# Sample rows of retention and state space laid out by head and token, and their state updates in sets of four

## What is computed

```python
def retention_chunk(S, q, k, v, log_gamma):            # 4 heads, dk = dv = 128, a state S for each sequence
    ...
    scores = jnp.einsum('bnhd,bmhd->bhnm', q, k) * decay[None]
    intra = jnp.einsum('bhnm,bmhe->bnhe', scores, v)
    cross = jnp.einsum('bnhd,bhde->bnhe', q * q_decay[None, :, :, None], S)
    S_new = jnp.exp(log_gamma * C)[None, :, None, None] * S + \
        jnp.einsum('bmhd,bmhe->bhde', k * k_decay[None, :, :, None], v)
    return S_new, intra + cross                         # then normalised per head, times silu(gate)

def ssd_chunk(h, x, dt, a, Bm, Cm):                     # 8 heads x 64, state 128
    ...
    cross = jnp.einsum('bnhs,bhps->bnhp', Cm, h) * jnp.exp(cum)[..., None]
    w = jnp.exp(cum[:, -1:] - cum) * dt
    h_new = jnp.exp(cum[:, -1])[:, :, None, None] * h + jnp.einsum('bmhp,bmhs->bhps', x * w[..., None], Bm)
    return h_new, intra + cross                         # then + D x, times silu(z), grouped RMSNorm
```

## Time and profile before

| what | value |
|---|---|
| time, median of 3 runs | 3921.76 us (3918.91 to 3924.99) |
| the profiled execution | 3920.59 us |
| its span, first to last instruction | 3918.7 us |
| TensorE busy, mean granted clock | 3511.9 us (90%), 0.931 |
| VectorE busy | 1735.5 us (44%) |
| ScalarE, GpSimd busy | 727.9 us (19%), 244.7 us (6%) |
| DMA | 365.8 MB, 93 GB/s over the span |

### The profile page before, as it was taken

The page is one execution under the profiler, slowest core; times in us unless marked ns, Lnnn a source line. Parts: engine busy times, 40 slices in busy tenths (PEclk is TensorE's granted clock), DMA queues, the critical chain, the costliest instruction groups (busy, mean ns, idle before and its releaser), DMA issues. The chain is left out here.

```text
span 3918.7 us, 45141 instructions
## 1 busy us (share of the span) xinstructions
PE 3511.9 (90%) x18090; PEld 2454.4 (63%) x18090; DVE 1735.5 (44%) x3249; ACT 727.9 (19%) x1550; POOL 244.7 (6%) x250
## 2 busy tenths in 40 slices
PE   5988899998988788999989889998988886989998
PEld 2643455576666566888846345555766674868887
DVE  2146295134545523454512653940445364144543
ACT  1222222111322200000012222221213221010000
POOL 0000321200100000000000004112000000000000
PEclk9989899888998889999999899997989997999999
DMA  3211355522314031222222114436231321212221
GB/s 118 86 60 39 109 180 169 179 88 91 108 39 131 25 100 44 86 86 70 70 93 92 39 49 153 159 134 223 83 111 55 96 66 57 87 47 82 86 78 64
DMA packets 274202, 365.83 MB, mean 93 GB/s; under 512 B 39006, under 2 KB 170462, under 8 KB 273860
## 3 DMA queue, kind: packets, MB, share of 16 engines
q1 hardware_dynamic: 231580, 260.59, 20.4%
q0 software_dynamic: 21504, 75.51, 6.0%
q10 hardware_dynamic: 20904, 26.78, 1.9%
HBM read 312.50 MB, written 50.34 MB: 93 GB/s over the span
## 5 line engine op out<-in xcount | busy, mean ns | idle before, releaser
L382 PE MATMUL ps<-hT,ring 128*128 128x272 f32 x3072 | 784.7, 411 | 81.4 <-PEq L154 54.8
L382 PEld LDWEIGHTS ps<-hT,ring 128*128 128x128 f32 x3072 | 596.8, 199 | 232.4 <-issue 77.0
L374 PE MATMUL ps<-ring,hT 128*128 128x512 f32 (+3 forms) x1600 | 656.8, 552 | 35.1 <-DVE hT L637 19.0
L374 PEld LDWEIGHTS ps<-ring,hT 128*128 128x128 f32 (+1 forms) x1600 | 279.7, 199 | 325.9 <-issue 301.6
L382 PE MATMUL ps<-branchT,ring 128*128 128x272 f32 x1024 | 271.5, 421 | 31.7 <-DVE arena L492 22.8
L2468 PE MATMUL ps<-hT,ring 128*128 128x272 f32 x1136 | 278.7, 396 | 17.4 <-DVE hT L637 17.4
L382 PEld LDWEIGHTS ps<-branchT,ring 128*128 128x128 f32 x1024 | 203.9, 204 | 93.2 <-DVE arena L492 27.6
L2468 PEld LDWEIGHTS ps<-hT,ring 128*128 128x128 f32 x1136 | 217.7, 192 | 63.5 <-issue 18.2
L961 DVE MAX8 branchT<-arena 32x8 f32<-32x2080 f32 x64 | 148.2, 2316 | 2.2
L962 DVE MATCH_REPLACE8 arena<-branchT,arena 32x2080 f32<-32x2080 f32 x64 | 147.0, 2297 | 0.0
L2468 PE MATMUL ps<-arena,ring 128*128 128x272 f32 x528 | 126.4, 393 | 2.8 <-DMA ring<-in_w_down 2.8
(11 more groups left out here) (465 smaller groups left out, 4455.5 us busy)
## 6 DMA issues: line engine op xcount, KB each, us to landing
ring<-in_w_in SPq DMA_DIRECT2D x44, 2048.0 KB, 8.1
ring<-in_w_gu SPq DMA_DIRECT2D x44, 1024.0 KB, 6.5
spill<-stage ACTq DMA_DIRECT2D x72, 256.0 KB
arena<-spill SPq DMA_DIRECT2D x16, 1024.0 KB, 5.6
ring<-in_w_branch SPq DMA_DIRECT2D x16, 1024.0 KB, 5.3
ring<-in_w_down SPq DMA_DIRECT2D x8, 1536.0 KB, 6.6
ring<-in_w_down SPq DMA_DIRECT2D x8, 1280.0 KB, 5.8
ring<-in_w_out SPq DMA_DIRECT2D x4, 2048.0 KB, 9.8
```

Source lines behind the costliest of these rows:

```text
L374: mm = pe.matmul(bank[0:m, 0:w], hT[:, c, t0:t0 + m], slot3(j)[:, c, 0:w], start=(c == 0), stop=(c == kn - 1))
L382: mm = pe.matmul(bank[:, 0:HALF], slot3(j)[:, c, at:at + P], src, start=(c == 0), stop=(c == kn - 1))
```

## The change

Both sample tiles get a row for each head and token.

In retention the values and gates are loaded again by SyncE in that layout (`v_ht`, `g_ht`, eight loads of 32 by 128); k is turned as a whole by one product and scaled by a constant column (`rk_ht`) into `kds`; the queries of all heads are masked in one operation, the values spread in one. The four heads' row products go to four groups of 32 partitions of one bank. The norm runs on 128 partitions by 128. The state updates follow the turning of the rows and come in two sets (sequences 0 to 3, 4 to 7), each of four products from four groups of 32 rows into banks 0, 1, 4, 3. The stage's last sharing point lies between the sets.

In the state space x, B and the decay weights of the sample tokens are turned by products with the identity into four groups of partitions, copied by ScalarE (`qt`) and weighted by VectorE (`xw_qt`). GpSimd takes over the multiplication of the states by their decays. The updates follow the turning of the rows, in the same two sets with the last sharing point between; the norm chain stays at 32 by 512.

The diff, cut (what is removed stands in full in the functions above):

```diff
+    put("rk_ht", np.stack([np.exp(g * (TS - 1.0 - ts)) * sc for g in lg]).reshape(P, 1))
...
+            v_ht, g_ht = ar.take(P), ar.take(P)
...
+            qm = brT_[:, 8 * T + 2048:8 * T + 3072].rearrange("p (b n) -> p b n", b=NB)
+            kds = kT[:, P:2 * P]
+            added = (0, 1, 4, 3)
...
-                        if last:
...
-                                mm = pe.matmul(o, qT[:, h * m:h * m + m], Sp[:, h, :], start=False, stop=True)
...
                             mm.then_inc(S("b_out"), 1)
                             turn(i + 1)
                         else:
+                            pe.wait_ge(S("b_prompt_state"), 1)
+                            pe.transpose(ps[4][:, 0:P], kT[:, 0:P], ident).then_inc(S("b_k_turned"), 1)
+                            pe.wait_ge(S("b_state_in"), 64)
+                            pe.wait_ge(S("b_q_masked"), 1)
                             for h in range(4):
-                                pe.wait_ge(S("b_v_masked"), h + 1)
...
-                                              Vx[0:NS, half * 4:half * 4 + 4, :].rearrange("p b e -> p (b e)")).then_inc(S("b_state_add"), 1)
+                                pe.matmul(ps[3][h * NS:h * NS + NS, 0:P], A[0:NS, h * NS:h * NS + NS], v(4)[0:NS, h * P:h * P + P], start=True, stop=False)
+                            for b in range(NB):
+                                for h in range(4):
+                                    mm = pe.matmul(ps[3][h * NS:h * NS + NS, 0:P], qm[:, b, h * NS:h * NS + NS], S0[:, b, h, :], start=False, stop=(b == NB - 1))
+                            mm.then_inc(S("b_rows_out"), 1)
                         share.point("pe", pe)
                         share.point("pe", pe)
                         pe.wait_ge(S("b_y"), i + 1)
-                        for h in range(4):
...
-                        share.point("pe", pe)
+                        if not last:
...
+                        else:
+                            pe.transpose(ps[2][:, 0:P], t2[:, 0:P], ident).then_inc(S("b_y_turned"), 1)
+                            pe.wait_ge(S("b_v_spread"), 1)
+                            pe.wait_ge(S("b_kd"), 1)
+                            for half in range(2):
+                                for h in range(4):
+                                    if half:
+                                        pe.wait_ge(S("b_state_new"), h + 1)
+                                    r = slice(h * NS, h * NS + NS)
+                                    pe.matmul(ps[added[h]][:, :], kds[r], Vx[r, half * 4:half * 4 + 4, :].rearrange("p b e -> p (b e)")).then_inc(S("b_state_add"), 1)
+                                if half == 0:
+                                    share.point("pe", pe)
+                        if not last:
+                            share.point("pe", pe)
...
-                            for h in range(4):
...
-                                                             ALU.mult, ALU.add).then_inc(S("b_state_new"), 1)
+                            dve.tensor_tensor(qm.rearrange("p b (h t) -> p b h t", h=4), bc(qT[:, 0:P].rearrange("p (h t) -> p h t", h=4), 1, NB),
+                                              bc(msk, 2, 4), ALU.mult).then_inc(S("b_q_masked"), 1)
+                            dve.wait_ge(S("b_rows_in"), 16 * 8)
+                            dve.tensor_tensor(Vx, bc(v_ht, 1, NB), bc(K("hsel"), 2, P), ALU.mult).then_inc(S("b_v_spread"), 1)
+                            dve.wait_ge(S("b_k_turned"), 1)
+                            dve.tensor_scalar(kds, ps[4][:, 0:P], K("rk_ht"), None, ALU.mult).then_inc(S("b_kd"), 1)
+                            dve.wait_ge(S("b_rows_out"), 1)
...
+                        nh = 1 if last else 4
+                        rows = lambda a: a[:, 0:nh * P].rearrange("p (h d) -> p h d", h=nh)
+                        o, y, w, mean, sq = rows(ps[3]), rows(t2), rows(t1), sm[:, 0, 0:nh], sm[:, 1, 0:nh]
...
-                        dve.tensor_tensor(t2[0:m, :], t2[0:m, :], g(i)[0:m, :], ALU.mult).then_inc(S("b_y"), 1)
+                        L(dve, dve.tensor_tensor(y, y, bc(sq, 2, P), ALU.mult))
+                        dve.tensor_tensor(t2[:, 0:nh * P], t2[:, 0:nh * P], g_ht if last else g(i), ALU.mult).then_inc(S("b_y"), 1)
                         share.point("dve", dve)
-                        share.point("dve", dve)
+                        if last:
+                            for half in range(2):
+                                for h in range(4):
+                                    dve.wait_ge(S("b_state_add"), 4 * half + h + 1)
+                                    st = S0[:, half * 4:half * 4 + 4, h, :]
+                                    dve.scalar_tensor_tensor(st, st, GAMMA[h] ** TS, ps[added[h]][:, :].rearrange("p (b e) -> p b e", b=4),
+                                                             ALU.mult, ALU.add).then_inc(S("b_state_new"), 1)
+                                if half == 0:
+                                    share.point("dve", dve)
+                        else:
+                            share.point("dve", dve)
...
+                            for dst, row in ((v_ht, 2), (g_ht, 3)):
+                                for h in range(4):
+                                    sp.dma_start(dst[h * NS:h * NS + NS, :], spill[row, SEQ:T, h * P:h * P + P]).then_inc(S("b_rows_in"), 16)
...
+            qt = xn2[:, 1, 0:258]
+            xw_qt = xn2[:, 1, 384:512]
+            added = (0, 1, 4, 3)
...
+                @block.gpsimd
+                def _(pool):
+                    pool.wait_ge(S("ssm_in"), 64)
+                    pool.wait_ge(S("ssm_decays"), 1)
+                    pool.wait_ge(S("hs_turned"), 8)
+                    for half in range(2):
+                        for q in range(4):
+                            st = h0[:, half * 4:half * 4 + 4, q, :]
+                            pool.tensor_tensor(st, st, bc(dec[:, q, half * 4:half * 4 + 4], 2, P), ALU.mult).then_inc(S("ssm_decayed"), 1)
...
                             mm.then_inc(S("d_out"), 1)
+                            for q in range(4):
+                                r = slice(q * NS, q * NS + NS)
+                                pe.matmul(ps[0][r, 0:P], xc[:, q, SEQ:T], ident)
+                                pe.matmul(ps[0][r, P:2 * P], xc[:, 4 + q // 2, SEQ:T], ident)
+                                mm = pe.matmul(ps[0][r, 2 * P:2 * P + 2], ident[0:NS, 0:NS], wt[0:NS, 2 * q:2 * q + 2])
+                            mm.then_inc(S("d_rows"), 1)
...
-                            for n in range(8):
...
-                                          Bx[0:NS, half * 4:half * 4 + 4, :].rearrange("p b s -> p (b s)")).then_inc(S("ssm_add"), 1)
...
+                        if last:
+                            pe.wait_ge(S("b_spread"), 1)
+                            pe.wait_ge(S("ssm_decays"), 1)
+                            for half in range(2):
+                                for q in range(4):
+                                    if half:
+                                        pe.wait_ge(S("ssm_new"), q + 1)
+                                    r = slice(q * NS, q * NS + NS)
+                                    pe.matmul(ps[added[q]][:, :], xw_qt[r], Bx[r, half * 4:half * 4 + 4, :].rearrange("p b s -> p (b s)")).then_inc(S("ssm_add"), 1)
+                                if half == 0:
+                                    share.point("pe", pe)
+                        else:
+                            share.point("pe", pe)
...
+                            act.wait_ge(S("d_rows"), 1)
+                            act.activation(qt, ps[0][:, 0:258], ACT.Copy).then_inc(S("d_rows_taken"), 1)
...
+                            dve.wait_ge(S("d_rows_taken"), 1)
+                            dve.tensor_tensor(xw_qt.rearrange("p (x d) -> p x d", x=2), qt[:, 0:P].rearrange("p (x d) -> p x d", x=2), bc(qt[:, 2 * P:2 * P + 2], 2, 64), ALU.mult)
                             dve.wait_ge(S("ssm_decays"), 1)
                             dve.wait_ge(S("hs_used"), 8)
-                            for n in range(8):
...
-                            dve.wait_ge(S("ssm_new"), 8)
+                            dve.tensor_tensor(Bx, bc(qt[:, P:2 * P], 1, NB), bc(K("hsel"), 2, P), ALU.mult).then_inc(S("b_spread"), 1)
...
+                        if last:
+                            for half in range(2):
+                                for q in range(4):
+                                    n = 4 * half + q
+                                    dve.wait_ge(S("ssm_add"), n + 1)
+                                    dve.wait_ge(S("ssm_decayed"), n + 1)
+                                    st = h0[:, half * 4:half * 4 + 4, q, :]
+                                    dve.tensor_tensor(st, st, ps[added[q]][:, :].rearrange("p (b s) -> p b s", b=4), ALU.add).then_inc(S("ssm_new"), 1)
+                                if half == 0:
+                                    share.point("dve", dve)
+                        else:
```

(14 more changed lines are left out.)

58 lines of the change are left out of this document (10 added, 48 removed).

## The result

The changed kernel takes 3856.7 us (median of 4 runs, 3851.8 to 3863.6) against 3923.4 us for the kernel before, measured beside it (4 runs, 3918.9 to 3929.6). The ratio is 0.983, with a 95% interval from 0.981 to 0.985. The forecast was 3868 us, in a range of 3846 to 3888: the sign and the range held, and the gain was larger than the 52.6 us forecast: 66.7 us by the medians, 61.9 by the profiled executions.

A forecast was written before the change was run, and what follows sets the result against it. TensorE's program order, filler queued behind waits, was taken to cost the time, not the amount of work. 2 x (20 + 6.3) = 52.6 us off 3920.6 us gave 3868 us, range 3846 to 3888 us.

The forecast's parts named there:

- Retention, 20 us a layer: Retention's sample tile: cheaper row and state products and earlier filler save 20 us a layer.
- The new bank wait: Retention's last filler: its second product waits 1.4 us for a bank VectorE frees behind four state adds and one take.
- The small loads: Retention: SyncE issues eight small loads of values and gates in 3.7 us, with nothing on the path.
- The two rivals without overlap: Four sets a layer run one after another, 3900 us, 4%; no column group overlaps either, 3960 us, 3%.
- The state space, 6.3 us a layer: State space stage: next stage starts at 1391.1 in place of 1397.4, 6.3 us saved a layer.
- The contention: State space norm chain: six operations with both inputs in SBUF slowed beside GpSimd's decays, 5.3 us a layer.
- The turned rows: State space start: TensorE turns x, B and decay weights into rows, shifting all that follows by 3.2 us.
- The gap at each change of shape: State space row turning: weight load idle 0.20 us when product shapes alternate, eight gaps a layer.
- The rival without contention: State space tail: GpSimd doesn't hold VectorE up, 5.3 us more gain a layer, 3857 us; chance 17%.
- The term of 6.0 us: State space end: the prompt store's issue ends 6.0 us after the first store's issue, between 5.0 and 8.8 us.
- The rival that the stores eat the gain: State space end: prompt's store still held 8.8 us, rows cost 4.3 us, stage saves 2.4 us, 3876 us; chance 15%.
- A clear: Gap between stages: clearing a semaphore name costs an estimated 0.07 us; three more names in retention cost 0.2 us.

The follow-up runs named there:

- with the last load held: Changed kernel with only the very last weight load of retention and of the state space issued after the state updates, ahead of the state store: 3872.2 us, ratio 0.987.
- a kernel that holds none: Changed kernel with the decays of the state space's sample states on ScalarE instead of GpSimd, no weight load held: 3858.8 us, ratio 0.984.
- shared clears: Changed kernel with each stage's semaphores cleared by all five engines, a fifth of the names each, instead of all by SyncE: 3846.9 us, ratio 0.982.
- the state space's part alone: Kernel before with only the state space hunks of the change, retention as before: 3906.9 us, ratio 0.996.

## Why the prediction was right, and where its sizes were off

1. **Retention, 20 us a layer: right.** It was 21.8 and 21.9 us in one execution, 20.0 and 21.9 in the other. Rows, sets and gap came within 0.5 us of their prices. The new bank wait is real, but 0.87 us and not 1.4: four adds took 2.48 us, where I had 4 x 0.69. Undoing it shortens the stage by 1.2 us a layer, though the one execution gave them back in HGRN2. I charged 0.5 us for half clock behind the stage; the clock there was 0.50 in the first 3.6 us of HGRN2, but its cost can't be told apart in that stage's spread. The small loads took 4.98 us to issue and not 3.7, and SyncE's next DMA left 32 us after they were out: hidden, as forecast.
2. **The four groups run side by side: shown**, by 1.95 against 7.17 us and 1.14 against 3.72. The two rivals without overlap fall. By 3.72 / 1.14 packing is worth 3.3 times in the state products, a little less than my 3.5. The Trainium skill's page TensorE: Matmul & The Clock Gate, Part 3, gives 3.07 times for four row groups; the runs here show somewhat more.
3. **The state space, 6.3 us a layer: mis-sized, 9.6 measured.** Three terms of the sum were too dear. The contention cost 3.55 us where I had 5.3: I priced each of the six operations with both inputs in SBUF at 0.88 us more, but they showed 0.84, 0.31, 0.73, 0.73, 0.67 and 0.25. The turned rows moved the decays by 2.3 us where I had 3.2. What follows them was 0.9 us shorter than priced, half of it in the second set (1.72 us and not 2.2). These are 1.8 + 0.9 + 0.9 = 3.6 us too many, against 3.3 missing; the stage ran 0.4 us late before the turning began. The 3.3 us and retention's 1.8 make some 10 us over two layers. The median came out 11 us below the forecast, though attention and HGRN2 moved by several microseconds of their own, in opposite directions. The gap at each change of shape is 0.20 us, as estimated:

```profile
1324.25 0.13 PEld L2210 LDWEIGHTS ps<-arena,cst 32*32 32x32 f32 x2 [0.20 <-issue]
```

4. **GpSimd holds VectorE up: shown**, by taking its work away and by giving it to ScalarE. The rival without contention falls.
5. **The stores.** The term of 6.0 us from the first store to the end of the prompt's issue was 5.8, and what sets it, the load's lead, is shown by holding the load. The rival that the stores eat the gain falls, but the store does end the stage: moved ahead, it is worth 4 us a layer.
6. **Missed: HGRN2 and attention.** I predicted nothing for untouched stages. HGRN2's tile load did issue sooner (3.39 us instead of 6.71). But with retention as before and the issue at 6.68 us, HGRN2 was shorter still, and with the last load held it came out hardly longer than in a kernel that holds none. So its 2.3 us can't be put down to the load; the last section says what it moves with. A clear comes to some 0.047 us and not 0.07, which left the sum as it was, since the gaps themselves came from rows.

## What to carry to other kernels

Four groups paid 3.3 times on products of 32 rows and 3.7 times on products of 32 columns, where neighbours in the order lie in different groups; HGRN2's timeline had shown both prices beforehand. When work moves to an idle engine, look at where the operands of its neighbour lie: beside GpSimd, VectorE's operations took up to 2.5 times as long where both inputs lay in SBUF (1.11 us instead of 0.44) and no longer where one lay in a bank; beside ScalarE they took no longer. And read small edits by the length of their stage, in more than one layer and execution.

## What the runs showed of the hardware that I had not expected

A stage's length moves with where TensorE's clock falls, in the same code. HGRN2 took 182.3 to 192.2 us in kernels whose HGRN2 is the same and whose last load is not held; 1.1 us of it are the shared clears. The two layers of one execution, in windows of the kernel with shared clears:

```profile
964.50:1146.80 182.30, 164.68 (x1618) 116.13 (x1618) 96.72 (x268) 56.57 (x101) 22.30 (x18) 0.97 0.25 74
2849.00:3040.30 191.30, 172.36 (x1618) 120.71 (x1618) 97.12 (x268) 56.57 (x101) 20.87 (x18) 0.93 0.23 71
```

Length times clock is nearly the same, 176.8 and 177.9; in the kernels above that hold no load it lies between 175.8 and 178.7 in every layer, with a clock of two digits. Attention moves too: with the same code up to there, and unchanged clears, layer 0's retention began between 805.3 and 813.4 us. One place where the clock falls is a pause of 3.7 us on TensorE ahead of HGRN2's fourth tile. Behind it the clock is at its lower level (1.2 GHz) for a while, by these windows to some 6.2 us behind the restart in the kernel before (first) and to 3.0 us in the one with the state space's part alone (second):

```profile
1085.32 3.09 PE L382 MATMUL ps<-branchT,ring 128*128 128x272 f32 x6 [3.70 <-DVE arena L492]
...
1088.00:1090.00 2.00, 2.00 (x7) 1.24 (x6) 0.00 (x0) 0.60 (x1) 0.00 (x0) 0.50 0.00 0
1090.00:1092.00 2.00, 2.00 (x5) 0.77 (x3) 0.31 (x1) 0.60 (x1) 0.00 (x0) 0.62 0.00 0
```
```profile
1088.01 3.09 PE L382 MATMUL ps<-branchT,ring 128*128 128x272 f32 x6 [3.70 <-DVE arena L492]
...
1088.80:1090.80 2.00, 2.00 (x6) 1.41 (x5) 0.00 (x0) 0.00 (x0) 0.00 (x0) 0.50 0.03 8
1090.80:1092.80 2.00, 2.00 (x9) 1.01 (x7) 0.00 (x0) 0.92 (x2) 0.00 (x0) 0.94 0.00 0
```

What sets the length of the low stretch, no run here tells.
